# Reordering five waits of an S5 and attention kernel, and 34 products of constants ahead of TensorE's first tile

## The reference

```python
# first block: Mamba-like scan (SSD), gated linear recurrence (RG-LRU), attention to a memory
h = rms_norm(x, norm_g); proj = h @ w_in
merged = g0 * (y_ssd @ w_br_ssd) + g1 * (y_lru @ w_br_lru) + g2 * (y_mem @ w_br_mem)
x = rms_norm(x + merged @ w_out, final_g)
# second block: four layers, x = x + rmsnorm(branch(rmsnorm(x, pre[i])), post[i])
#   0: S5. u, z = h @ w_in; complex diagonal scan over u in 64 groups of 16; gelu, glu; (y * silu(z)) @ w_out
#   1: sliding window. 16 heads of 64, window 128, relative bias, a sink per head; (o * silu(z)) @ w_out
#   2: latent attention. 16 heads, keys and queries of 64 + 32 rotated, from latents of 256 and 768;
#      causal softmax over 512 keys; (o * silu(z)) @ w_out
#   3: gated spatial unit, causal 128x128 mixing per group
```

## Time and profile before

| | us |
|---|---|
| median of 3 timed runs | 1905.64 |
| lowest, highest | 1905.22, 1906.73 |
| the profiled execution, its own time | 1907.74 |
| its span, first to last instruction | 1906.0 |
| TensorE busy | 1860.0 |
| VectorE, ScalarE, GpSimd busy | 1249.5, 904.5, 472.8 |

### The profile page before, as it was taken

The page is one execution under the profiler, slowest core; times in us unless marked ns, Lnnn a source line. Parts: engine busy times, 40 slices in busy tenths (PEclk is TensorE's granted clock), DMA queues, the critical chain, the costliest instruction groups (busy, mean ns, idle before and its releaser), DMA issues.

```text
span 1906.0 us, 26095 instructions
## 1 busy us (share of the span) xinstructions
PE 1860.0 (98%) x10128; PEld 1510.4 (79%) x10128; DVE 1249.5 (66%) x1925; ACT 904.5 (47%) x1563; POOL 472.8 (25%) x506
## 2 busy tenths in 40 slices
PE   7999999999999999999999999999999999999998
PEld 5787877888667888968899787888787866688877
DVE  7998785647559336555467855778668467649364
ACT  5546877311288214442243254547545555545332
POOL 0492110574358504024123621020001200000000
PEclk9999999999999999999999999999999999999999
DMA  4236542335222535525626934521133411124221
GB/s 169 86 102 195 164 145 80 113 122 185 96 81 89 166 111 166 200 79 174 198 83 181 225 99 109 125 76 56 56 101 110 137 45 34 34 89 142 91 77 67
DMA packets 70875, 222.16 MB, mean 117 GB/s; under 512 B 17105, under 2 KB 17793, under 8 KB 69729
## 3 DMA queue, kind: packets, MB, share of 16 engines
q1 hardware_dynamic: 43056, 157.83, 25.0%
q0 software_dynamic: 24240, 55.79, 10.4%
q10 hardware_dynamic: 3456, 6.87, 1.3%
HBM read 203.23 MB, written 14.81 MB: 114 GB/s over the span
## 4 chain that ended last, share of the span: by engine, by line
PE 85%; DVE 9%; ACT 3%; issue 2%; DMA 1%; DVEq 0%; POOL 0%; SPq 0%; ACTq 0%
PE bank L489 24%; PE bank L491 23%; PE bank L490 23%; DVE ring_low L451 2%; PE bank L3697 1%; PE bank L2151 1%; PE bank L3730 1%; PE bank L1075 1%; PE bank L2158 1%; PE bank L2351 1%; PE bank L2324 1%; DVE lru_x L2252 1%; ACT ring_high L446 1%; DVE sq L706 1%; PE bank L3469 1%
## 5 line engine op out<-in xcount | busy, mean ns | idle before, releaser
L451 DVE TENSOR_TENSOR ring_low<-ring,ring_high 128x1024 fp32r<-128x1024 f32 x283 | 391.1, 1393 | 261.4 <-ACT ring_high L446 260.9
L446 ACT ACTIVATE ring_high<-ring 128x1024 fp32r<-128x1024 f32 x283 | 297.2, 1056 | 520.1 <-PE bank L491 519.6
L489 PE MATMUL bank<-h_high,ring_high 128*128 128x512 f32 (+1 forms) x1276 | 503.9, 395 | 19.6 <-DVE ring_low L826 11.5
L491 PE MATMUL bank<-h_high,ring_low 128*128 128x512 f32 (+1 forms) x1276 | 491.2, 385 | 0.0
L490 PE MATMUL bank<-h_low,ring_high 128*128 128x512 f32 (+1 forms) x1276 | 491.1, 385 | 0.0
L489 PEld LDWEIGHTS bank<-h_high,ring_high 128*128 128x128 f32 x1276 | 241.0, 189 | 83.0 <-issue 30.7
L490 PEld LDWEIGHTS bank<-h_low,ring_high 128*128 128x128 f32 x1276 | 241.1, 189 | 48.5 <-issue 3.1
L491 PEld LDWEIGHTS bank<-h_high,ring_low 128*128 128x128 f32 x1276 | 240.8, 189 | 48.3
L489 PE MATMUL bank<-gated_high,ring_high 128*128 128x512 f32 (+1 forms) x240 | 85.4, 356 | 1.5 <-DVE gated_low L3299 1.1
L491 PE MATMUL bank<-gated_high,ring_low 128*128 128x512 f32 (+1 forms) x240 | 83.3, 347 | 0.0
L490 PE MATMUL bank<-gated_low,ring_high 128*128 128x512 f32 (+1 forms) x240 | 83.3, 347 | 0.0
(11 more groups left out here) (570 smaller groups left out, 3732.3 us busy)
## 6 DMA issues: line engine op xcount, KB each, us to landing
ring<-slabs SPq DMA_DIRECT2D x289, 512.0 KB, 3.3
acs_rows<-acs_rows POOLq DMA_DIRECT2D x16, 512.0 KB, 4.4
s_outputs<-s_ca POOLq DMA_DIRECT2D x4, 1152.0 KB, 5.3
x<-xT SPq DMA_DIRECT2D x2, 2048.0 KB, 8.8
exp_acs<-acs_rows POOLq DMA_DIRECT2D x16, 256.0 KB, 10.0
s_b<-s_br POOLq DMA_DIRECT2D x8, 512.0 KB, 4.3
s_rows<-s_powers POOLq DMA_DIRECT2D x16, 256.0 KB, 7.0
s_inputs<-s_w POOLq DMA_DIRECT2D x8, 512.0 KB, 3.6
```

Source lines behind the costliest of these rows:

```text
L446: act.activation(self.ring_high[:, self.splits_before[s] % AHEAD, :], self.ring[:, s % RING, :], ACT.Copy)\
L451: dve.tensor_tensor(self.ring_low[:, s % RING, :], self.ring[:, s % RING, :], self.ring_high[:, self.splits_before[s] % AHEAD, :].bitcast( ...
L489: pe.matmul(out, w[0], x[0], start=start, stop=False, **flags)
L491: return pe.matmul(out, w[1], x[0], start=False, stop=stop, **flags)
```

## The change

TensorE's program gets 34 plain fp32 products of `C.ones` with itself, 128 by 128 by 128, into the first 128 columns of the first tile's bank, behind the opening of the banks and ahead of the first real product. Nobody reads their result; the first real product has start=True.

In S5, ScalarE copies only tiles 0 and 2 of the second half, and computes the root after them; VectorE copies tiles 1 and 3 with a multiply, ahead of its reciprocal. In the sliding-window attention VectorE helps with the copies in the last pair only, and ScalarE does all four of the last but one. In the latent attention, the counter `pvd` is replaced by `first_half`, raised by the last value product of the even head; the last one of the odd head raises `bank_full` itself, and TensorE waits for neither. VectorE and ScalarE wait for both in front of the copies of the next pair. VectorE does the probabilities of head 15 ahead of the gate product at h = 14. ScalarE does the exponentials of head 1 ahead of the slab split, and the first curve after the copies of head 0.

```diff
@@ -781,6 +781,8 @@
             seen = set()
             for u in us:
                 C.open(pe, u)
+            for _ in range(34):
+                pe.matmul(C.bank[us[0].b][:, 0:P], C.ones[:], C.ones[:], start=True, stop=True)
             for k in range(KD):
                 if k == 5:
                     norm.sum_total(pe)
@@ -2972,6 +2974,10 @@
             for use in ends.values():
                 C.split_low(dve, use)
             C.split_low(dve, us[-1])
+            for t in (1, 3):
+                C.full(dve, us[t])
+                dve.tensor_scalar(L.UT[:, 32:64, t, :], C.bank[us[t].b][:].rearrange("p (g h) -> p g h", g=32),
+                                  entry.token_root(dve, t), None, ALU.mult).then_inc(C.bank_read[us[t].b], 1)
             entry.root_on_dve(dve, total)
 
         @block.scalar
@@ -2987,12 +2993,15 @@
                     entry.token_root_on_act(act, rows)
                 if half == 1:
                     C.split_high(act, us[-1])
-                    entry.root_on_act(act, total)
                 for t, u in enumerate(us):
+                    if half == 1 and t % 2:
+                        continue
                     C.full(act, u)
                     act.activation(L.UT[:, 32 * half:32 * half + 32, t, :], C.bank[u.b][:].rearrange("p (g h) -> p g h", g=32),
                                    ACT.Copy, scale=entry.token_root(act, t))\
                         .then_inc(C.bank_read[u.b], 1)
+                if half == 1:
+                    entry.root_on_act(act, total)
                 if half == 0:
                     C.split_high(act, first_z[0])
                     C.full(act, kb[-1])
@@ -3545,7 +3554,7 @@
                     gated(j - 1)
                 if j + 1 < NJ:
                     probs(j + 1)
-                if j >= NJ - 2:
+                if j == NJ - 1:
                     copies(j)
                 if j + 2 < NJ:
                     logits(j + 2)
@@ -3582,7 +3591,7 @@
             curve(0)
             for j in range(NJ):
                 for n, u in enumerate(pb[j]):
-                    if j >= NJ - 2 and n % 2:
+                    if j == NJ - 1 and n % 2:
                         continue
                     C.full(act, u)
                     lo = 0 if n else 1
@@ -3678,7 +3687,7 @@
             ob.append(C.take_given(7))
     C.pinned = ()
     ex, pn = C.reserve("ex", H), C.reserve("pn", H)
-    kt_, pvd, scd = C.reserve("ktile", 2 * 8 + 4), C.reserve("pvd", H), C.reserve("scd", H)
+    kt_, first_half, scd = C.reserve("ktile", 2 * 8 + 4), C.reserve("first_half", H // 2), C.reserve("scd", H)
     K0 = 4
     gate = L.gate
     with C.stage() as block:
@@ -3730,9 +3739,10 @@
                             mm = pe.matmul(C.bank[u.b][64 * e:64 * e + 64, kt * P:T], L.V[:, kt, 64 * g:64 * g + 64],
                                            key_block(g, kt), start=(kt == 0), stop=(kt == TC - 1))
                             if kt == TC - 1:
-                                mm.then_inc(pvd.sem, 1)
-                    pe.wait_ge(pvd.sem, pvd.at(h))
-                    pe.sem_inc(C.bank_full[u.b], 1)
+                                if e == 0:
+                                    mm.then_inc(first_half.sem, 1)
+                                else:
+                                    mm.then_inc(C.bank_full[u.b], 1)
 
         @block.vector
         def _(dve):
@@ -3767,6 +3777,7 @@
 
             def gated(i):
                 u = ob[i]
+                dve.wait_ge(first_half.sem, first_half.at(i))
                 C.full(dve, u)
                 dve.wait_ge(gate.factor.sem, gate.factor.at(i))
                 dve.scalar_tensor_tensor(out=L.Y[:, i, :], in0=C.bank[u.b][:], scalar=0.5, in1=L.Z[:, i, :], op0=ALU.mult,
@@ -3783,12 +3794,13 @@
             evac_z(0)
             spent = zb[0][0]
             for h in range(H):
+                if h == H - 2:
+                    probs(h + 1)
                 if h > 0 and h % 2 == 0:
                     gated(h // 2 - 1)
-                if h == H - 2:
-                    probs(h + 1)
                 if h > 1:
-                    dve.wait_ge(pvd.sem, pvd.at(h - h % 2 - 1))
+                    dve.wait_ge(first_half.sem, first_half.at(h // 2 - 1))
+                    C.full(dve, ob[h // 2 - 1])
                 for kt in (1, 3):
                     u = pb[h][kt]
                     C.full(dve, u)
@@ -3858,16 +3870,18 @@
             keys(0)
             exps(0)
             keys(2)
+            exps(1)
             C.split_high(act, zb[0][0])
-            exps(1)
-            curve(0)
             for h in range(H):
                 if h > 1:
-                    act.wait_ge(pvd.sem, pvd.at(h - h % 2 - 1))
+                    act.wait_ge(first_half.sem, first_half.at(h // 2 - 1))
+                    C.full(act, ob[h // 2 - 1])
                 for kt in (0, 2):
                     u = pb[h][kt]
                     C.full(act, u)
                     act.activation(key_block(h, kt), C.bank[u.b][:, kt * P:T], ACT.Copy).then_inc(C.bank_read[u.b], 1)
+                if h == 0:
+                    curve(0)
                 if h + 2 < H:
                     exps(h + 2)
                     if h % 2 and h + 3 < H:
```

## The result

| | before | after |
|---|---|---|
| median, us | 1906.18 (4 executions beside the change) | 1897.02 (1896.5 to 1897.94) |
| profiled execution, its own time | 1907.74 | 1897.37 |
| its span | 1906.0 | 1895.6 |
| TensorE busy | 1860.0 | 1865.6, the 34 products included |

The ratio is 0.9948, interval 0.9934 to 0.9961: 0.5% faster, well past the 0.2% that can be told from no change. Predicted was 1895.0 with a range of 1891.8 to 1899.5. TensorE's lines of the changed kernel are two higher after the start and nine higher from S5 on (L3061 is L3070, L3469 is L3478, L3697 is L3706, L3714 is L3723, L3730 is L3739); those of the other engines are up to twelve higher.

The account below looks back on a forecast made before the run. TensorE, busy 98% of the span, was taken as the bound. Terms of 9.7 us, or 11.55 with 1.85 for the clock, took the median from 1905.64 to 1895.9 or 1894.1; the middle, 1895.0, was forecast, range 1891.8 to 1899.5.

Parts of the forecast that it names:

- Start: Start of the kernel: 34 products of constants let the first real products run at full pace, 1.7 us gained (0.8 to 1.95).
- the cap of VectorE's additions: Start: the sum of squares needs VectorE's additions, which end at 25.65, so at most 1.95 us can be gained.
- S5: S5 transpositions: root after ScalarE's copies and half the copies on VectorE bring TensorE's second group earlier, 0.95 us (0.6 to 1.4).
- Sliding-window attention: Last two pairs there: VectorE without pair 6's copies makes pair 7's earlier, shortening TensorE's two waits, 1.2 us (0.7 to 2.2).
- First head: First head of the latent attention: ScalarE's copies come earlier, removing TensorE's 2.07 wait and drain overlap, 2.3 us (2.0 to 2.4).
- Self-waits: Latent attention, odd heads: TensorE no longer waits for its own value products, 0.4 us each, 2.8 in all (1.6 to 4.0).
- Last head: Head 15 of the latent attention: VectorE's probabilities ahead of the gate product come 0.75 us earlier (0.5 to 1.3).
- Clock: Last pair's value products, latent attention: no half-clock stretch after the shortened wait, 1.85 us, or 0 if it stays.
- A: Start: the constants do not raise the clock, all 34 cost 0.43 us, -5.15 instead of +1.7; 1901.9 us, chance 0.06.
- C: Start: the 34 products do not overlap in their one bank, 0.55 us each, 11.7 late; 1909.3 us, chance 0.03.
- B: After the start: removed waits come back as others, half of the 8.0 us is lost; 1899.0 us, chance 0.12.
- D: Other executions may also fall to the lower clock at the 2.07 and 2.2 us waits; 1891 to 1892 us, chance 0.05.

Follow-up runs that it names:

- the filled waits: Kernel before with products of constants (13, 9, 9 and 8) in four of TensorE's waits, no wait removed: 1905.63 against 1906.78 us.
- the change again: The changed kernel unaltered, measured once more against the kernel before: 1898.32 against 1905.94 us, ratio 0.9957.
- the moved coefficients: Changed kernel with ScalarE's S5 exponential and sines behind the slab's high part, VectorE's steps for them one tile later: 1898.13 against 1898.32 us.

## Why the prediction was right, and where its terms were off

- **Start, 1.7.** Right at the mark of the sum of squares: 1.91 in this profile, 1.7 by the means of six and six. That it reaches the end is read from the stretches behind it, which repeat; the medians don't resolve it. Two errors cancelled. The constants stayed at half clock until 6.0, not for the 5.16 us that I had copied from the first real group, so they ended at 11.4 and not 12.1; and the cap of VectorE's additions, which I had "only just" not binding, bound.
- **S5, 0.95.** 1.15, or 1.08 alone. The timeline shows the parts:

```profile
1028.88 1.40 DVE L2979 TENSOR_SCALAR u_tok<-bank,st 128x512 f32<-128x512 f32 x2
1028.91 3.07 PE L3070 MATMUL bank<-ident,u_tok 128*64 128x64 f32 x96 [0.35 <-ACT u_tok L3000]
...
1030.20 3.34 DVE L1750 RECIPROCAL norm_root<-norm_root 128x512 f32<-128x512 f32 x1
...
1031.81 1.11 PE L3083 MATMUL bank<-u_chunks,s_wv 128*64 128x64 f32 x32
...
1033.62 0.69 DVE L3152 TENSOR_TENSOR s_p<-bank,s_rot 128x512 f32<-128x512 f32 x1
```

  The third group runs on without the 0.1 that I took off. The 1.95 of idle time ahead of VectorE's multiply did not quite cover its two copies: the products that feed it start at 1031.81 and the multiply at 1033.62, 1.81 later, where before it was 1.25 (1034.78 and 1036.03). So VectorE alone is 0.56 late, for which I had 0.3, and TensorE loses nothing by it. I had not looked at the scan behind it, where transfers set the pace and scatter by more than this gain.
- **Sliding-window attention, 1.2.** 1.17, which no run has alone: it is the mark F, 245.64 to 245.74 in all profiles with this edit. The first wait, 2.21, is gone altogether, and the second has grown from 0.74 to 1.66, where I had 1.9 for both. VectorE's copies of pair 7 are the wait that is left:

```profile
1356.03 1.29 DVE L3543 COPY swa_pt<-bank 128x512 f32<-128x512 f32 x2
...
1356.78 1.58 PE L3478 MATMUL bank<-swa_pt,swa_v 128*64 128x128 f32 x24 [1.66 <-DVE swa_pt L3543]
```

- **First head, 2.3.** 2.35, the wait and the overlap behind it, as worked out.
- **Self-waits, 2.8.** Mis-sized: 2.05. The step "0.34 idle plus about 0.07 of overlap" fails, since each brought its idle time and no more. The last one, 0.4, brought nothing, since the copies are late in its place (2.93 for the sixteen). The Trainium skill ("TensorE: Matmul & The Clock Gate", Part 2) has the weights of coming products loaded while the present one runs; the price that I had drawn from it for a wait would have given 3.5; 0.34 each, the idle time alone, speaks against that price here.
- **Last head, 0.75.** 0.80 in J, but this is for the order and the seventh self-wait together, for which I had 1.15. The wait for head 15 is 1.38, predicted about 1.5.
- **Clock, 1.85.** 1.70 in the profile, so the size is right, but I had tied it to the code. It is a draw at every long wait: at 2.07 us two profiles fell and two did not. What I put into the median for it, half of 1.85, is near the 1.15 that the filled waits gave, by luck.
- **Sum.** 9.4 on the marks without the clock, against 9.7; 11.1 with it, against 11.55; less 0.57 in the scan and 0.2 elsewhere. The median came out 2.0 above my 1895.0. Of that, 0.5 is the median of before, 1906.18 with one execution more where I had 1905.64, 0.3 the terms, perhaps 0.4 the scan (60.8 against 60.5 in the means), and some 0.8 I can't assign; the interval of the ratio is 2.6 us wide to either side.
- **Rivals.** A and C fell with the first window. B, removed waits come back as others, is right in small: 0.4 at the last pair, 0.35 at head 15, not half. D had the right mechanism, falls at 2.07 and 2.2 us in other executions, and a gain that is mostly in the spread. C's "0.58 us a product" follows from no number of its working, which has 0.55, and 1.1 at the lower clock.

## What to carry to other kernels

Before costing a wait, mark ten or so fixed points and compare the stretches between them over several executions: that separates what an edit does (most stretches here repeat to 0.1 us) from the clock's draws (0.5 to 1.7) and the transfers' (up to 2.4), which a median of a few runs mixes. A wait on the engine that bounds the kernel costs its length and, sometimes, a stretch at half clock behind it; filling it with idle products protects from the second, but wins only where no other engine sets the next mark. Products that warm the clock have to reach to the real work: seventeen that ended 4.3 us early show no gain. Each one beyond that is paid in full.

## What the runs showed of the hardware

- Falls to 1.2 GHz after waits of TensorE. Ahead of 62.8 to 69.0 (3.1 to 3.2 us) nine profiles fell and one, the change again, did not; 2.2 in the window attention, three of five (F above 247.2); 2.07 at the first head, two of four; 1.8 to 2.2 ahead of head 15, three of four; with the moved coefficients 2.58 at 81.4, two of two, and 1.62 at 61.2, none of one; 1.66 in the changed window attention, none of eight; 1.38 to 1.40 in the changed latent attention, none of nine; 1.41 for u_tok in the old code, none of five. The same wait in the same code can go either way.
- The windows read 1.00 for the clock during the first microseconds in every profile while the pace is that of 1.2 GHz, with products of constants (0.43) as with real ones. The record behind them has its first entry only where the pace changes: 16.57 before, 5.88 after. A fall behind that it does show, as in the run with 17 constants, 0.50 from 11.7 to 14.4. The Trainium skill ("TensorE: Matmul & The Clock Gate", Part 1) warns that such records are not to be trusted alone; up to the first entry the trace agrees with that, and after 64 us record and pace agree with each other.
- When the clock first rises differs between executions: between 4.9 and 7.9 us with the constants starting at 2.07 in each of eight profiles, between 15.5 and 17.4 with the first products at 11.3 to 11.5 in each of six.
- An fp32 product of `C.ones` with itself, 128x128x128, takes 0.22 us from start to start at 2.4 GHz and 0.43 at 1.2; into the same 128 columns of one bank they run without a stall.
